# Prompt attention and decode scores of eight paged sequences in one interleaved order, with keys transposed in place

## The reference, cut to what matters

```python
qp, kp, vp = attn_qkv(np_in, pos_p, b_w_qkv[j], b_q_norm[j], b_k_norm[j])   # 8 heads, 4 key/value heads, 128 wide
op = moba_attention(qp, kp, vp, pos_p)                                      # prompt: causal over 256 tokens
qs, ks_new, vs_new = attn_qkv(ns_in, pos_s, ...)
past_k = cache_k[j][page_table].reshape(bs, past_len, N_KV_HEADS, HEAD_DIM) # 8 pages of 128 rows per sequence
past_v = cache_v[j][page_table].reshape(bs, past_len, N_KV_HEADS, HEAD_DIM)
os_ = moba_attention(qs, concat(past_k, ks_new), concat(past_v, vs_new), pos_s)
# moba: four past blocks of 256 rows; the three with the highest q . mean(k) take part, and the own block
ms = os_.reshape(bs, ts, N_HEADS * HEAD_DIM) @ b_w_o[j]
```

## Time and profile before

| | us |
|---|---|
| Runs shown | 815.23, 816.61, 808.06 |
| Median | 815.23 |
| Profiled execution, its own time | 814.83 |
| Its span in the trace | 813.1 |
| PE busy | 646.9 (80% of the span) |
| DVE, ACT, POOL busy | 291.7, 160.1, 138.6 |
| DMA | 187.77 MB, mean 231 GB/s |
| Mean granted TensorE clock | 0.902 of full |

### The profile page before, as it was taken

One profiled execution on the slowest core, in us unless ns is written; L12 is line 12 of the kernel. 1 busy time (PEld: TensorE's weight loads), 2 busy tenths in 40 slices (PEclk: granted clock), 3 DMA queues, 4 the chain that ended last, 5 costly groups with the idle time before them and its releaser, 6 DMA issues.

```text
span 813.1 us, 12476 instructions
## 1 busy us (share of the span) xinstructions
PE 646.9 (80%) x4123; PEld 443.2 (55%) x4123; DVE 291.7 (36%) x916; ACT 160.1 (20%) x336; POOL 138.6 (17%) x224
## 2 busy tenths in 40 slices
PE   5899999848998883799988857675996698898850
PEld 3677667535555542576667526444774455564520
DVE  2202211373424321547747431323016524324314
ACT  2114101111212211111124321211112212222200
POOL 0000000011332320131114001420000132332222
PEclk9999959978999997799999986965998699999985
DMA  9864300315996994980019563874805099699933
GB/s 343 286 238 191 135 27 1 154 68 196 413 409 228 414 401 148 405 312 0 1 63 370 175 212 121 321 259 194 336 30 210 17 400 413 251 405 414 410 146 121
DMA packets 58153, 187.77 MB, mean 231 GB/s; under 512 B 11996, under 2 KB 12558, under 8 KB 53766
## 3 DMA queue, kind: packets, MB, share of 16 engines
q1 hardware_dynamic: 46598, 158.71, 51.0%
q0 software_dynamic: 11520, 28.60, 9.5%
HBM read 182.95 MB, written 13.76 MB: 242 GB/s over the span
## 4 chain that ended last, share of the span: by engine, by line
PE 67%; DVE 11%; DMA 10%; issue 5%; ACT 3%; SPq 3%; DVEq 0%; POOLq 0%; ACTq 0%
PE PS L1007 24%; PE PS L1092 14%; PE PS L1110 7%; DMA ew_in<-in_moe_w_up 5%; PE PS L998 3%; PE PS L1303 2%; DMA half_a<-in_cache_k 2%; PE PS L1267 2%; DMA zT<-y_rows 2%; PE PS L1178 2%; PE PS L1023 1%; PE PS L1063 1%; SPq L292 1%; DVE zT L850 1%; PE PS L1175 1%
## 5 line engine op out<-in xcount | busy, mean ns | idle before, releaser
L1092 PE MATMUL PS<-ew_in,zT 128*64 128x256 f32 x832 | 99.2, 392 | 7.5 <-DMA ew_in<-in_moe_w_up 4.3
L1007 PE MATMUL PS<-hT,half_a 128*128 128x288 f32 x384 | 98.1, 414 | 4.0 <-DVE hT L680 3.1
L1092 PEld LDWEIGHTS PS<-ew_in,zT 128*64 128x64 f32 x832 | 67.9, 142 | 46.2 <-issue 27.6
L1007 PEld LDWEIGHTS PS<-hT,half_a 128*128 128x128 f32 x384 | 73.1, 193 | 27.8 <-issue 3.7
L850 DVE SCALAR_TENSOR_TENSOR zT<-PS,slot_gates,zT 64x256 f32<-64x256 f32 x34 | 16.5, 485 | 147.9 <-ACT zT L582 143.6
L1007 PE MATMUL PS<-hT,half_b 128*128 128x288 f32 x256 | 65.7, 416 | 3.3 <-DVE hT L680 3.3
L1110 PE MATMUL PS<-ew_down,zT 128*64 128x512 f32 x208 | 50.4, 601 | 14.5 <-issue 14.5
L1007 PEld LDWEIGHTS PS<-hT,half_b 128*128 128x128 f32 x256 | 49.3, 194 | 19.1 <-issue 3.7
L494 POOL DMA_INDIRECT y_rows<-zT,out_idx x34 | 34.3, 1010 | 147.7 <-ACT zT L585 147.7
L1267 PE MATMUL PS<-cst,half_a 128*128 128x128 f32 x256 | 39.5, 304 | 19.5 <-DMA half_a<-in_cache_k 11.9
L1267 PEld LDWEIGHTS PS<-cst,half_a 128*128 128x128 f32 x256 | 31.0, 153 | 35.7 <-issue 18.9
(11 more groups left out here) (234 smaller groups left out, 908.5 us busy)
## 6 DMA issues: line engine op xcount, KB each, us to landing
ew_in<-in_moe_w_gate SPq DMA_DIRECT2D x26, 1024.0 KB, 7.1
ew_in<-in_moe_w_up SPq DMA_DIRECT2D x26, 1024.0 KB, 9.7
ew_down<-in_moe_w_down SPq DMA_DIRECT2D x26, 1024.0 KB
half_a<-in_cache_k SPq DMA_DIRECT2D x64, 256.0 KB, 3.8
ew_in<-in_cache_v POOLq DMA_DIRECT2D x32, 256.0 KB, 6.9
half_b<-in_cache_v POOLq DMA_DIRECT2D x32, 256.0 KB, 5.8
half_a<-in_a_w_in SPq DMA_DIRECT2D x1, 4096.0 KB, 15.4
half_b<-in_a_w_in SPq DMA_DIRECT2D x1, 4096.0 KB, 25.5
```

Of the source, the lines that this page charges most:

```text
L1007: mm = pe.matmul(PS[:, bank, 0:T], w[:, k, col:col + P], src[:, k, :], start=(k == 0), stop=(k == KT - 1))
L1092: mm = pe.matmul(PS[f * SLOT:(f + 1) * SLOT, 2 + u, 0:EF], x_slotsT[:, u, k % 4, k // 4, :], w_in[u][:, f, k, :], start=(k == 0), stop=(k ...
```

## The change

Buffers are named by homes: `c0`, `c1` (the two `ew_in`), `d` (the two `ew_down` together), `b0`, `b1`, `a0`, `a1` (the halves of `half_b` and `half_a`). `K_HOME` and `V_HOME` say where each of the eight sequences' keys and values lie. The qkv weights are loaded in four quarters into b0, b1, a0 and a1, the output weights in two halves into b0 and b1.

Key pages are issued by SP, the first three sequences right behind the qkv weights, the next four as each quarter of the qkv projection is over. A transposed page is copied from PSUM over the page itself, and the score matmuls read the transposed page there. The value pages are issued by SP too: sequence b waits for the scores of sequences up to b + 1, the last one for the first values. POOL issues no pages.

One loop of 18 iterations on PE, DVE and ACT takes four key pages, one unit of prompt attention (now a key/value head with its two query heads, by chunk: eight units) and the decode scores of the half before it. DVE adds the causal mask. Score banks of the two groups are different (6 and 7, 2 and 3), and so are `PdT`, `new_part`, `q_pad` and the statistics. Group 0's softmax, its probability transposes and its new rows stand inside the loop; group 1's softmax follows it, and on PE three sequences of values of group 0 stand ahead of group 1's probability transposes. The probabilities of past keys are no longer scaled; the output copy on ACT scales.

The homes, and SP:

```diff
-            load(w_b, w_qkv[:, :, 0:D], S["w_q_in"])
-            load(w_a, w_qkv[:, :, D:2 * D], S["w_kv_in"])
-            for u in range(2):
-                expert_down(1, u, ew_down[u], E[1][f"wd{u}"])
+            for u in range(4):
+                load(w_qkv_at[u], w_qkv[:, :, u * HALF:(u + 1) * HALF], s_home[QKV_HOME[u]][0])
...
+        K_HOME = ("c0", "c1", "d", "b0", "b1", "a0", "a1", "c0")
+        V_HOME = ("c1", "d", "b0", "b1", "a0", "a1", "c0", "c1")
...
             sp.wait_ge(S["pages_in"], 16)
-            hold(S["qkv"], 2 * KT)
-            for b in range(2):
-                sequence(sp, b, k_pages[:, b], ck, s_k[b])
-
-            sp.wait_ge(S["kvt_sb"], 2 * NT)
+            for b in range(3):
+                sequence(sp, b, K_HOME[b], ck)
+            for b in range(3, 7):
+                sp.wait_ge(S["qkv"], 4 * (b - 2))
+                sequence(sp, b, K_HOME[b], ck)
+            sp.wait_ge(S["kvt_sb"], NT)
+            sp.wait_ge(S["vtok_sb"], 3 * NT)
...
-            with sp.Fori(1, NB // 2) as pair:
-                for u in range(2):
-                    sequence(sp, 2 * pair + u, k_pages[:, u], ck, s_k[u],
-                             lambda n: hold(S["kt"], 1 + (2 * pair + u - 2) * NPAGE + n))
-            sp.wait_ge(S["kt"], 1 + NB * NPAGE)
-            load(w_a, t["b_w_o"][0].rearrange("(k p) n -> p k n", p=P), S["w_o_in"])
+            sp.wait_ge(S["sc"], 2)
+            sequence(sp, 7, K_HOME[7], ck)
+            for b in range(NB):
+                if b < 7:
+                    sp.wait_ge(S["sc"], 2 * (b + 2))
+                else:
+                    sp.wait_ge(S["pv"], 1)
+                sequence(sp, b, V_HOME[b], cv)
+            w_o = t["b_w_o"][0].rearrange("(k p) n -> p k n", p=P)
             for u in range(2):
-                sp.wait_ge(S["pv"], 1 + NB - 1 + u)
+                sp.wait_ge(S["pv"], 3 + u)
+                load(w_o_at[u], w_o[:, :, u * HALF:(u + 1) * HALF], s_home[O_HOME[u]][0])
+            sp.wait_ge(S["pv"], 6)
+            prefetch(1, 0)
+            for u in range(2):
+                sp.wait_ge(S["pv"], 7 + u)
                 expert_in(1, u, ew_in[u], E[1][f"w{u}"])
+                expert_down(1, u, ew_down[u], E[1][f"wd{u}"])
```

On POOL:

```diff
-            for b in range(2, GRP):
-                sequence(pool, b, v_pages[b], cv, [s_v[b]] * 2)
+            pool.memset(q_pad[0], 0.0).then_inc(S["q_set"], 1)
...
+            for g in range(NG):
+                if g == 1:
+                    pool.wait_ge(S["kvt"], NT)
+                    pool.memset(q_pad[1], 0.0).then_inc(S["q_set"], 1)
+                pool.wait_ge(S["q_set"], 2 + g * (GRP + 1))
                 for bb in range(GRP):
+                    q = qs[:, (g * GRP + bb) * QC:(g * GRP + bb + 1) * QC].rearrange("p (a r) -> p a r", a=KV)
+                    pool.tensor_copy(q_pad[g][:, bb, :, bb * G * TS:(bb + 1) * G * TS], q).then_inc(S["q_set"], 1)
```

On ACT:

```diff
+            def key_page(n):
+                act.wait_ge(S["kt"], n + 1)
+                act.copy(page_rows(K_HOME[n // NPAGE], n % NPAGE), PS[:, 1, :]).then_inc(S["kt_act"], 1)
...
+            for i in range(NHF + 2):
+                if i < NHF:
+                    key_page(4 * i + 1)
...
+                if i == PARTS + 1:
+                    past_probs(0)
+                if i == PARTS + 4:
+                    past_probs_up(0)
+            past_probs(1)
+            past_out(0)
+            past_probs_up(1)
+            past_out(1)
```

On DVE:

```diff
+            def past_stats(g, part):
+                scores = PS[:, SC_BANK[g] + part, :].rearrange("p (b n) -> p b n", n=MOBA_BLOCK)
+                dve.wait_ge(S["sc"], (g + 1) * PARTS - 1 + part)
+                dve.tensor_reduce(dst[:, g, 2 * part + 4:2 * part + 6], scores, AX.X, ALU.max)
+                link(dve.tensor_reduce(dst[:, g, 2 * part:2 * part + 2], scores, AX.X, ALU.add))
...
+            for i in range(NHF + 2):
+                if i < NHF:
+                    key_page(4 * i)
...
+                u = i - 1
+                if 0 <= u < NU:
...
+                    dve.wait_ge(S["ps"], u + 1)
+                    link(dve.tensor_tensor(both[:, :, c * P:w], both[:, :, c * P:w], causal_neg.unsqueeze(1).to_broadcast([P, G, P]), ALU.add))
+                    link(dve.tensor_reduce(stat[:, 0, u, :], both, AX.X, ALU.max))
+                    dve.tensor_scalar(stat[:, 1, u, :], stat[:, 0, u, :], -SCALE, None, ALU.mult).then_inc(S["pneg"], 1)
+                if i == PARTS + 1:
+                    past_stats(0, 1)
+                if i < NHF:
+                    key_page(4 * i + 2)
...
+                if i == PARTS:
+                    past_stats(0, 0)
+                if i == PARTS + 1:
+                    past_bias(0)
+                if i == PARTS + 2:
+                    past_sums(0)
+                if i == PARTS + 4:
+                    past_probs_up(0)
```

On PE:

```diff
+            def key_page(n):
+                if n % 4 == 0:
+                    b = n // NPAGE
+                    pe.wait_ge(*landed(K_HOME[b], n // 4 % 2, turn[b]))
+                upto(pe, S["kt_act" if n % 2 else "kt_dve"], n // 2)
+                page = page_rows(K_HOME[n // NPAGE], n % NPAGE)
                 for a in range(KV):
...
+                    mm = pe.transpose(PS[:, n % 2, a * P:(a + 1) * P], page[:, a * P:(a + 1) * P], ident)
+                mm.then_inc(S["kt"], 1)
...
+            def past_scores(hf):
...
+                pe.wait_ge(S["kt_dve"], 2 * hf + 2)
+                pe.wait_ge(S["kt_act"], 2 * hf + 2)
+                keys = homes[K_HOME[hf // 2]][part].rearrange("p (j a n) -> p j a n", j=NPAGE // 2, a=KV)
+                for a in range(KV):
+                    mm = pe.matmul(PS[a * HR:(a + 1) * HR, SC_BANK[g] + part, :], q_pad[g][:, bb, a, :], keys[:, :, a, :],
+                                   start=(bb == 0), stop=(bb == GRP - 1))
+                mm.then_inc(S["sc"], 1)
...
+            for i in range(NHF + 2):
+                if i < NHF:
+                    key_page(4 * i)
+                    key_page(4 * i + 1)
...
+                    for k in range(G):
+                        mm = pe.matmul(PS[:, 2 + u % 2, k * w:(k + 1) * w], zT[:, G * a + k, c * P:w], zT[:, NH + a, 0:w],
+                                       start=True, stop=True)
...
+                if i < NHF:
+                    key_page(4 * i + 2)
+                    key_page(4 * i + 3)
+                if 1 <= i <= NHF:
+                    past_scores(i - 1)
...
+                if i == PARTS + 4:
+                    past_probs_up(0)
+                if i == PARTS + 5:
+                    new_values(0)
+            for b in range(GRP - 1):
+                past_values(b)
+            past_probs_up(1)
+            past_values(GRP - 1)
+            new_values(1)
+            past_values(GRP)
+            past_rows(0)
+            for b in range(GRP + 1, NB):
+                past_values(b)
+            past_rows(1)
             pe.wait_ge(S["pv_sb"], NG * GRP)
-            pe.wait_ge(S["w_o_in"], 16)
-            project(KT, hT, 4)
+            for u in range(2):
+                home, tiles_before = O_HOME[u], landed(O_HOME[u], 0, 2)[1]
+                pe.wait_ge(s_home[home][0], tiles_before + 16)
+            project(KT, lambda ob: (w_o_at[ob // 4], (ob % 4) * P), hT, 4)
```

More of the change, by code:

```diff
@@ L267, in hybrid_step @@
         QUADS = 2
-        DSTEPS = 13
         def source_ready(eng, n, k):
@@ L655, in _ @@
-                act.activation(Pn[:, :], Sn[:, :], ACT.Exp, bias=dst[:, 15:16], scale=SCALE,
-                               accum_out=dst[:, 28:29]).then_inc(S["dexp"], 1)
-                act.wait_ge(S["dpt"], g + 1)
-                act.copy(PdT[:, 0:4, :].rearrange("p j c -> p (j c)"), PS[:, 0, :]).then_inc(S["dpt_act"], 1)
-                act.wait_ge(S["pv"], 1 + (g + 1) * GRP)
-                act.copy(o_rows, PS[:, 5, :]).then_inc(S["o_sb"], 1)
+                    act.activation(Pd[:, w], scores[:, w], ACT.Exp, bias=dst[:, g, 16 + k:17 + k], scale=SCALE,
+                                   accum_out=dst[:, g, 24 + k:25 + k]).then_inc(S["dexp"], 1)
@@ new lines, in past_probs, with past_probs_up, past_out @@
+                act.activation(Pn[:, :], Sn[:, :], ACT.Exp, bias=dst[:, g, 15:16], scale=SCALE,
+                               accum_out=dst[:, g, 28:29]).then_inc(S["dexp"], 1)
+            def past_probs_up(g):
+                act.wait_ge(S["dpt"], g + 1)
+                act.copy(PdT[g][:, 0:4, :].rearrange("p j c -> p (j c)"), PS[:, (4, 0)[g], :]).then_inc(S["dpt_act"], 1)
+            def past_out(g):
+                act.wait_ge(S["pv"], (g + 1) * GRP)
+                act.activation(o_rows[g], PS[:, SC_BANK[g], :], ACT.Identity, scale=dst[:, g, 33:34]).then_inc(S["o_sb"], 1)
@@ new lines, in new_out, with past_rows @@
+            def new_out(g):
+                dve.wait_ge(S["new_v"], g + 1)
+                link(dve.tensor_copy(new_part[g][:, :], PS[:, (7, 3)[g], P:2 * P]))
+            def past_rows(g):
```

(24 more changed lines are left out.)

421 lines of the change are left out of this document (202 added, 219 removed).

## The result

The changed kernel took **771.81 us** (median of 4 runs, 770.15 to 774.77) against 813.05 us for the kernel before (4 runs, 808.06 to 816.61): ratio 0.9501, 95% interval 0.9437 to 0.9565. That is 41 us less; 780 had been forecast, in a range of 762 to 803. The profiled execution took 770.98 us (span 769.1, mean clock 0.914).

A forecast was written before the change was run, and what follows sets the result against it. Serial order and late pages bound the attention stage; SP's issuing would bound it next. Output weight at 540.6, equivalent projection start 542.4 instead of 575.2, 32.8 us less: 814.8 - 32.8 = 782, put at 780, range 762 to 803.

The forecast's parts named there:

- SP as the bound: Attention stage: SP's page issuing, not transfer, is slower; 9.1 us a sequence, 45.5 us for values of sequences 3 to 7.
- The output weight behind V7 as the last wait: End of attention stage: output weight, queued on SP after the last value pages, ends last, at 540.6 us.
- Score 10: New loop: tenth decode score, carrying group 0's softmax, ends at 481.2 us, after seven prompt iterations of 5.2 us.
- The output weight: Before the output projection: two halves, 0.5 + 0.5 + 12.9 us from SP's turn at 526.7 to landing at 540.6.
- The slow start: Start of output projection: PE, having stood still, starts slowly and loses 1.8 us, giving an equivalent start of 542.4.
- the last stretch: End of the kernel, after the projection: durations held equal, everything after the projection's start shifting as a whole.
- rival A: Attention stage: SP keeps up and the compute chain ends it at 526 to 531; 766 to 771 us; chance 0.17.
- The scores' end: Attention stage: after six more halves, with group 0's transposes and new rows between, decode scores end at 505 us.
- the computation's end: Attention stage: compute chain of softmax, values and rows ends at 531 us, or 534, before the output weight lands.
- B: New loop: interleave gives nothing within an iteration, 6.75 us instead of 5.2; 793, up to 803 us; chance 0.24.
- C: New loop: PE runs at its lower clock level, 9.2 us per iteration instead of 5.2; 833 us; chance 0.06.
- D: Key pages under the qkv stage: early pages do not come early, nothing gained; 807 to 823 us; chance 0.08.

The follow-up runs named there:

- experiment 9: Changed kernel with page numbers of value sequences 3 to 7 read ahead of the key pages, and each output weight half awaited at first use: 762.69 us, ratio 0.9387.
- experiment 7: Changed kernel with GpSimd issuing even value sequences, output weight halves awaited at first use, and expert weights held until the output weight landed: 763.27 us, ratio 0.9400.
- experiment 5: Changed kernel with the output weight's two halves issued by GpSimd instead of SyncE, behind the same waits: 774.66 us, ratio 0.9535.
- experiment 4: Changed kernel with value pages of sequences 1, 3, 5 and 7 issued by GpSimd instead of SyncE, same waits: 770.54 us, ratio 0.9462.
- experiment 2: Changed kernel with no key page asked for before the last qkv projection is done (about 418 us): 819.77 us, ratio 1.0118.
- experiment 8: Changed kernel with GpSimd issuing even value sequences and output weight halves awaited at first use, expert weights not held back: 763.82 us, ratio 0.9412.
- experiment 6: Changed kernel with the output projection waiting for each half of the output weight at its first use, nothing else: 771.04 us, ratio 0.9494.

## Why the prediction was right

**SP as the bound: right, to the tenth.** V3 to V7 were put at 5 x 9.1 = 45.5 us; from 475.2 to 520.75 it is 45.5. The output weight behind V7 as the last wait: right. The prediction named reads and issues for 4.8 of the 9.1 us and put the rest down to register steps; experiment 9 shows that 4.3 of the 9.1 us go when the reads do.

**Score 10: too late by 6.0 us** (481.2 predicted, 475.2 measured), and that is the main error in the time. Three terms: the first scores end at 427.0 instead of 429.6 (-2.6), because the row transposes run beside the first halves and not ahead of them; seven iterations take 32.6 us instead of 36.4 (-3.8), 4.7 each, where 4.8 was the lower bound and 5.2 taken; the ninth and tenth together take 15.6 instead of 15.2 (+0.4), group 0's softmax holding up the copies as forecast. I added slack for engines waiting for each other; PE was 36.15 of 38.0 us busy and had none to add.

**The output weight: too short by 0.7 us.** From SP's turn to it to the first matmul 13.9 us were predicted, 14.6 measured. The expert weights, issued from 521.94, share the DMA engines with it (1.01 busy), but that they cause it is not shown: holding them back in experiment 7 gave nothing. **The slow start** was 2.9 us in the projection's first half (18.68 against 15.79), not 1.8. That the whole from the projection to the last matmul is nevertheless 0.4 us shorter than before is luck: the stretch from the projection's last block to the first expert, held equal in the prediction, is 3.0 us shorter, at a granted clock of 0.85 instead of 0.79 (stage rows, before and after):

```profile
604.38:642.59 38.21, 25.18 (x139) 17.76 (x137) 23.00 (x93) 10.26 (x19) 3.99 (x7) 0.79 0.32 119
...
567.49:602.75 35.26, 22.18 (x138) 16.37 (x137) 22.97 (x93) 10.07 (x19) 4.10 (x7) 0.85 0.35 129
```

**The sum.** The gain was put at 32.8 us against the profiled execution; between the spans it is 44.0. Of the 11.2 us of difference 5.2 are the start (540.6 predicted, 535.4 measured), 2.2 the slow start, charged with 1.8 but not to be found in the time from the projection to the last matmul, 0.4 shorter than before, and 3.8 the last stretch, also held equal, of which 2.6 go with who issues the pages and 1.2 are within what runs differ by. All three made the kernel faster than forecast, so the measured time lies at the lower edge of the forecast's own 771 to 788 and 0.8 us above rival A's 771: by the time alone the two could not be told apart. SP's issues without a break and the output weight as the last wait decide it.

**The scores' end** was put at 505 and is 496.3 (the last row of L1328, from 494.38 for 1.92 us), and the computation's end at 531: in experiment 9, where PE waits for no page and no weight, the projection starts 102.6 us after qkv, at 520.9 on the clock of the changed kernel. Neither sets the time here.

**Rivals.** A: the computation and the bytes do end at +103 to +104 when SP keeps up (experiments 7 and 9), but SP does not keep up. The Trainium skill, in "DMA: Bandwidth & Descriptors", section "Issuing engines are not separate DMA queues", says that all DMAs share the same engines and that issuing from several saves only initiation time, usually small. The first half is what experiment 5 shows (weight earlier, pages later, start unchanged). The second does not fit a page of 256 KB here: 1.14 us to issue against an estimated 0.68 to move, at the 388 GB/s of experiment 4. B: 4.7 us an iteration, not 6.75; undoing the interleave, with the units ahead, costs 29 us. C: the loop's clock was 1.00; eight transposes took 1.04 to 1.09 us. The Trainium skill, in "TensorE: Matmul & The Clock Gate", section "Part 4: PE-mode transpose", says that the full clock does not engage in transpose mode; in this trace transposes do run at it (the granted clock of 1.00), but with other matmuls between them, and no run here tests transposes alone. D: the first six sequences of keys were early; experiment 2 shows the price if they had not been: 48 us.

## What to carry to other kernels

When many small transfers go through one issuing engine, add up that engine's own instructions (index read, register steps, issue) and set them against the transfer; here reading the indices ahead was worth as much as a second issuing engine (11.3 and 9.6 us of the stage, experiments 9 and 8 against 6). Once that is lifted, look at the next bound before promising the whole gain: in experiment 4 only 6 us of an expected 12 came, and in experiment 5 moving a transfer forward only pushed others back. Work that feeds a queue is worth what the queue's slack lets through, not its own length.

## What the runs showed of the hardware that was not expected

- A page issued by GpSimd costs as much as one by SyncE: 4.53 us for four (508.39 to 512.92), 1.13 each, table read included.
- When GpSimd has issued value pages, the span ends 7.98 to 8.06 us after the issue of the last output starts (five profiled runs), otherwise 5.40 to 5.60 (eight). That output itself lands 3.5 us after its issue both in the changed kernel and in experiment 4. The cause is open.
- PE stops without a wait that the profile shows, 2.47 us among V7's matmuls ahead of 522.38 in experiment 9, while expert weights are loading (DMA share 1.02 from 519.9 to 522.4), and 1.90 us ahead of 520.97 in experiment 8. The cause is open.
